# Expert weights in loads of 2 MB, a ring of eight homes and an activation in two halves, in a one-core streaming encoder step

## What is computed

```python
logits = h @ w_router + b_router
gates, experts = softmax_of_top4(logits)
for each expert e, for its tokens xe:
    gu = xe @ w_gate_up[e] + b_gate_up[e]          # (1024, 2048)
    g = jnp.minimum(gu[:, :1024], 7.0)
    u = jnp.clip(gu[:, 1024:], -7.0, 7.0)
    a = g * jax.nn.sigmoid(1.702 * g) * (u + 1.0)
    ye = a @ w_down[e] + b_down[e]                 # (1024, 1024)
x = x + sum over a token's experts of gate * ye
```

## Time and profile before

| | before |
|---|---|
| runs | 1434.07, 1432.60, 1427.69 us |
| median | 1432.6 us |
| the profiled execution's own time | 1428.79 us |
| its span | 1426.8 us |
| mean granted TensorE clock | 0.959 of full speed |
| PE / DVE / ACT busy | 1296.7 / 322.1 / 188.2 us |
| read from HBM | 439.24 MB |

### The profile page before, as it was taken

One profiled execution on the slowest core, in us unless ns is written; L12 is line 12 of the kernel. 1 busy time (PEld: TensorE's weight loads), 2 busy tenths in 40 slices (PEclk: granted clock), 3 DMA queues, 4 the chain that ended last, 5 costly groups with the idle time before them and its releaser, 6 DMA issues.

```text
span 1426.8 us, 15124 instructions
## 1 busy us (share of the span) xinstructions
PE 1296.7 (91%) x5759; PEld 597.6 (42%) x5759; DVE 322.1 (23%) x530; ACT 188.2 (13%) x344; POOL 34.5 (2%) x38
## 2 busy tenths in 40 slices
PE   5999996889988998999989899998999989899996
PEld 3445453774464434434343343434434344343432
DVE  1056004113032212312121221212312122221213
ACT  3120213220110111001010100101001010100100
POOL 4000004000000000000000000000000000000000
PEclk9999998989978999999999999999999999999999
DMA  9131421031734999999999999999999999999993
GB/s 309 59 118 59 139 83 47 2 125 61 307 129 171 379 416 411 415 410 407 410 405 416 412 414 406 406 416 419 415 420 411 413 404 416 410 414 407 403 416 141
DMA packets 89715, 443.10 MB, mean 311 GB/s; under 512 B 7971, under 2 KB 9787, under 8 KB 56414
## 3 DMA queue, kind: packets, MB, share of 16 engines
q1 hardware_dynamic: 85376, 434.94, 75.7%
q10 hardware_dynamic: 3054, 4.87, 1.0%
q0 software_dynamic: 1264, 2.99, 0.7%
HBM read 439.24 MB, written 3.53 MB: 310 GB/s over the span
## 4 chain that ended last, share of the span: by engine, by line
PE 71%; DVE 8%; issue 3%; ACT 1%; DMA 1%; DVEq 0%; SPq 0%; POOL 0%; PEldq 0%
PE bank L1385 31%; PE bank L1419 18%; PE bank L1365 7%; PE bank L1352 4%; PE bank L1237 3%; PE bank L1297 3%; DVE tu L992 1%; DVE tu L999 1%; DVE aT L1002 1%; PE bank L1406 1%; DVE tu L996 1%; DVE tg L985 1%; DMA wpool<-in_w_pool 1%; PE bank L1317 1%; PE bank L1249 1%
## 5 line engine op out<-in xcount | busy, mean ns | idle before, releaser
L1385 PE MATMUL bank<-near,xT 128*64 128x512 f32 x1280 | 284.4, 594 | 15.7 <-PE bank L1419 14.7
L1385 PEld LDWEIGHTS bank<-near,xT 128*64 128x64 f32 x1280 | 96.0, 137 | 198.7 <-issue 198.7
L959 DVE TENSOR_TENSOR x<-x,bank 128x512 f32<-128x512 f32 x102 | 70.1, 687 | 438.0 <-PE bank L1365 438.0
L1419 PE MATMUL bank<-ring,aT 128*64 128x512 f32 x768 | 168.3, 594 | 0.0
L1385 PE MATMUL bank<-ring,xT 128*64 128x512 f32 x768 | 167.5, 592 | 0.0
L1047 PE MATMUL bank<-ring,hT 128*128 128x512 f32 (+1 forms) x384 | 160.7, 578 | 1.6 <-DMA ring<-in_w_in 1.3
L1419 PE MATMUL bank<-near,aT 128*64 128x512 f32 x256 | 84.4, 821 | 45.3 <-DVE aT L1002 45.3
L1047 PEld LDWEIGHTS bank<-ring,hT 128*128 128x128 f32 x384 | 73.0, 192 | 85.5 <-issue 81.4
L1352 PE MATMUL bank<-pick,h 128*128 128x128 f32 x768 | 95.1, 282 | 9.1 <-PE bank L1385 5.9
L1385 PEld LDWEIGHTS bank<-ring,xT 128*64 128x64 f32 x768 | 55.2, 137 | 109.6 <-issue 109.6
L1352 PEld LDWEIGHTS bank<-pick,h 128*128 128x128 f32 x768 | 90.8, 197 | 22.7 <-issue 19.0
(11 more groups left out here) (247 smaller groups left out, 787.4 us busy)
## 6 DMA issues: line engine op xcount, KB each, us to landing
near<-in_w_gate_up SPq DMA_DIRECT2D x160, 1024.0 KB, 12.9
ring<-in_w_gate_up SPq DMA_DIRECT2D x96, 1024.0 KB, 9.8
ring<-in_w_down SPq DMA_DIRECT2D x96, 1024.0 KB, 12.2
near<-in_w_down SPq DMA_DIRECT2D x32, 1024.0 KB, 8.4
ring<-in_w_in SPq DMA_DIRECT2D x16, 1024.0 KB, 8.1
ring<-in_w_out SPq DMA_DIRECT2D x4, 1024.0 KB, 5.8
ring<-in_cache_k SPq DMA_DIRECT2D x2, 1024.0 KB, 6.7
ring<-in_cache_v SPq DMA_DIRECT2D x2, 1024.0 KB, 6.8
```

What stands on the lines that cost most here:

```text
L959: V.tensor_tensor(x[:, t, 512 * h:512 * h + 512], x[:, t, 512 * h:512 * h + 512], bank[6 + q % 2][:, :], ALU.add).then_inc(y_added, 1)
L1385: last = T.matmul(bank[n][64 * a:64 * a + 64, :], xT[:, w, 64 * a:64 * a + 64], slot_of(2 * w + a)[:, 512 * n:512 * n + 512], start=(w == ...
L1419: last = T.matmul(bank[4 + n][64 * a:64 * a + 64, :], aT[:, 2 * j + c, 64 * a:64 * a + 64], slot_of(k + a)[:, D * c + 512 * n:D * c + 512 ...
```

## The change

It does these things:

- **Loads.** A load is 2 MB: one piece of 16 KB per partition, for both kinds. For gate/up partition `p` gets rows 8p+2j and 8p+2j+1 (pieces of 16 KB that lie 64 KB apart in memory); for down it gets rows 4p to 4p+3 of a half (the 2 MB lie together). A pair has four gate/up steps `j` and two down steps `h`, for two experts: 12 loads.
- **Homes.** Eight homes of 2 MB: five in `near` and three in the old `ring`, and a sixth place in `near` that is used once, by load 8, since `g2row` and `sq2` stand there until the second norm is done. Six loads can go before the output projection is done, two after it, and load 8 after the norm. `unit_used` goes up by two per step, now 4 MB at a time.
- **Order of contraction.** `gather` takes the columns of `h2` with stride 8, the transposes take those of `gu` and `bgn` with stride 4, so that rows and weights meet.
- **Activation.** It is done in two halves of 512 columns; `aT` serves as the sigmoid's target too, and ACT copies three of the four banks. The last gate/up step computes its banks in the order 0, 2, 1, 3; the first transposes go before bank 3's matmuls. Each down step waits only for its own half.
- **Loop.** Turns stand in twos (`b`), the first two written out ahead of the loop. Ranks are kept once and lowered by 64 when used, in place of six copies.
- **The end.** The last two loads go in four pieces of 1 MB, by halves of the last down step. The last six combine matmuls go to banks of their own and wait for no add; `x` is written in six transfers of 256 KB. The router bias is fetched by ACT after `g2row` instead of by POOL at the start.

```diff
-DEPTH = 12
+DEPTH = 8
+LOADS = 24
+SCOL = 2 * 2048
+STREAM = [(b, j, a) for b in range(2) for j in range(6) for a in range(2)]
+GU_STEPS = 4
+        def place(k, first):
+            return k if first and k <= DEPTH else (k - 1) % DEPTH
...
+            def source(k, group, rows=4, row=0):
+                b, j, a = STREAM[k]
+                if j < GU_STEPS:
+                    return bass.AP(gu_t, group * (4 * D * 2 * FF) + ((2 * b + a) * (D * 2 * FF) + 2 * j * 2 * FF),
+                                   [[KC * 2 * FF, P], [1, SCOL]])
+                return bass.AP(dn_t, group * (4 * FF * D) + ((2 * b + a) * (FF * D) + (j - GU_STEPS) * (FF // 2) * D + row * D),
+                               [[4 * D, P], [1, rows * D]])
...
-            for k in range(DEPTH):
-                if k >= RING:
-                    sp.wait_ge(released, PRO_UNITS - RING + (k - RING) + 1)
-                load(k, 0)
+            for k in range(DEPTH + 1):
+                if 5 <= k < 8:
+                    sp.wait_ge(released, PRO_UNITS - RING + 2 * (k - 5) + 2)
+                if k == 8:
+                    sp.wait_ge(sumsq2, NT)
+                    sp.wait_ge(h2_ready, NT)
+                load(k, 0, True)
             sp.wait_ge(route_ready, 1)
             turns = turns_of(sp)
+            for k in range(DEPTH + 1, LOADS):
+                sp.wait_ge(unit_used, k - DEPTH if k <= 2 * DEPTH else k - DEPTH + 1)
+                load(k, 0, True)
...
+            for piece in range(2):
+                for a in range(2):
+                    k = LOADS - 2 + a
+                    sp.dma_start(slot_of(k, False)[:, piece * 2 * D:(piece + 1) * 2 * D],
+                                 source(k, PAIRS_E // 2 - 1, 2, 2 * piece)).then_inc(last_in[2 * piece + a], 16)
+            for q in range(2 * NT):
+                h, t = divmod(q, NT)
+                cols = slice(512 * h, 512 * h + 512)
+                dst = O[0][0, t * P:(t + 1) * P, cols] if t < 2 else O[1].rearrange("b s d -> (b s) d")[:, cols]
+                sp.wait_ge(x_done, q + 1)
+                sp.dma_start(dst, x[:, t, cols]).then_inc(out_sem, 16)
...
-                act.wait_ge(g_ready, i + 1)
-                act.wait_ge(table_set, i + 1)
-                A.activation(ts[:], tg[:], ACT.Sigmoid, scale=ALPHA).then_inc(sig_ready, 1)
-                if not final:
-                    gathered_out(i + 1, 1)
+                act.wait_ge(table_set, nth(1, 1))
+                for h in range(2):
+                    act.wait_ge(g_ready, nth(2, h + 1))
+                    A.activation(aT[:, 4 * h:4 * h + 4, :], tg[:, 4 * h:4 * h + 4, :], ACT.Sigmoid, scale=ALPHA).then_inc(sig_ready, 1)
+                    if not final:
+                        gathered_out(nth(1, 1), h)
...
-                                        h2[:, t, (4 * half + c) * P:(4 * half + c + 1) * P],
+                        last = T.matmul(bank[6 + half][:, c * P:(c + 1) * P], h2[:, t, 4 * half + c::KC],
```

More of the change, by code:

```diff
@@ L376, in _ @@
[L376 to L384, removed]
+                for k in range(LOADS):
+                    sp.wait_ge(unit_used, i * LOADS + (LOADS + k - DEPTH + 1))
+                    load(k, (i + 1) % (PAIRS_E // 2), False)
@@ L685, in _, with table_load @@
-            A.activation(table, eps, ACT.Sigmoid).then_inc(table_set, 1)
-            turn(turns, True)
+            def table_load():
+                A.activation(table, eps, ACT.Sigmoid).then_inc(table_set, 1)
+            for b in range(2):
+                table_load()
+                turn(0, 0, b, False)
+            with act.Fori(0, turns) as i:
+                for b in range(2):
+                    table_load()
+                    turn(i, 1, b, False)
+            for b in range(2):
+                table_load()
+                turn(turns, 1, b, b == 1)
@@ L931, in _ @@
             step(V.scalar_tensor_tensor(rt[:, 5, :], bank[0][:, 0:NT * E], 1.0, sel, ALU.add, ALU.mult))
-            for q in range(MAXPASS):
-                last = V.tensor_scalar(rank_all[:, q, :, :], rt[:, 5, :].rearrange("p (t e) -> p e t", t=NT), -float(q * SLOTS),
-                                       None, ALU.add)
-            step(last)
+            step(V.tensor_copy(rank[:], rt[:, 5, :].rearrange("p (t e) -> p e t", t=NT)))
             step(V.tensor_reduce(need, bank[0][:, 128:128 + E], AX.X, ALU.max))
@@ L1004, in _ @@
[L1004 to L1011 removed]
+                    dve.wait_ge(pickg_ready, nth(1, 1))
+                    pick_slots(nth(1, 1), following)
+                dve.wait_ge(gu_done, nth(4, 2))
+                V.tensor_copy(gu[:, FF:FF + 512], bank[2][:, :]).then_inc(gu_copied_v, 1)
@@ L1015, in _ @@
+            turn(turns, 1, 0, PAIRS_E // 2 - 1, PAIRS_E - 1, False)
+            turn(turns, 1, 1, PAIRS_E // 2 - 1, None, True)
         @block.tensor
@@ L1430, in turn @@
                         last.then_inc(back_turned, 1)
-                pe.wait_ge(down_done, 2 * i + 2)
-                pe.sem_inc(unit_used, 2)
+                if not final:
+                    pe.wait_ge(down_done, nth(2, 2))
+                    pe.sem_inc(unit_used, 2)
+                else:
+                    pe.wait_ge(back_ready, nth(1, 2))
+                    for q in range(6):
+                        h, t = divmod(q, NT)
+                        if q == 0:
+                            pe.wait_ge(rows_ready, nth(2, 3))
+                        if q == NT:
+                            pe.wait_ge(last_rows, 1)
+                        T.matmul(bank[LAST_BANKS[q]][:, :], back[:, t, :], y[:, 512 * h:512 * h + 512],
+                                 start=True, stop=True).then_inc(y_part, 1)
+            for b in range(2):
+                turn(0, 0, b, True, False)
             with pe.Fori(0, turns) as i:
-                turn(i, False)
-            turn(turns, True)
-            combine(turns + 1)
+                for b in range(2):
+                    turn(i, 1, b, False, False)
+            for b in range(2):
+                turn(turns, 1, b, False, b == 1)
 _CONSTANTS = {"c_keep": keep_constants, "c_mask": mask_constants, "c_rep": repeat_constants,
```

317 lines of the change are left out of this document (165 added, 152 removed).

## The result

The changed kernel takes **1448.6 us** (median of 4 runs, 1448.0 to 1450.1), the kernel before, measured beside it, 1430.5. The ratio is **1.0127** (95% interval 1.0109 to 1.0144): slower by 1.3%, where 1367 us and faster had been predicted. The profiled execution took 1448.01 us with a span of 1446.2 us, 19.4 longer than that of before. The mean granted clock rose from 0.959 to 0.977 of full speed, and the kernel still became slower.

A forecast was written before the change was run, and what follows sets the result against it. PE was taken as the bound, transfers keeping pace. Span 1426.8 − 40.1 − 3.6 − 23.8 + 4.8 + 1 − 1.9 + 2 = 1365.2 us, plus 2.0 outside it: 1367 us, range 1354 to 1390.

The forecast's parts named there:

- the predicted PE work: Expert loop: PE alone would need 57.2 us a turn after the change, less than the transfers need.
- The strided operands … So 0: Gathers and transposes on PE: loading weights with strides of 32 and 16 bytes adds 0, judged from transpose rows.
- The rival by strided weights: 64 strided PE records a turn take twice their 0.12 us: 7.7 us a turn longer, 1484 us; chance 0.01.
- Wait for `a_ready`, −40.1 us: PE's wait for the activation before down: halves remove it in fifteen turns, −40.1 us.
- The clock, −23.8 us: PE's granted clock in the loop: without the idle it no longer falls, fourteen turns × 1.70, −23.8 us.
- The rival that it falls "behind waits for data": PE's clock falls all the same, behind light gathers or data waits: 23.8 us back, 1389 us at most; chance 0.12.
- Three pieces, +0.3 us a turn: PE's transposes in a turn: one run of 16 becomes three pieces, 0.3 us a turn, +4.8 us in all.
- Routing and `bgn`, +1 us: Before the loop: fewer rank copies save about half a us, bgn's fetch beside expert loads costs +1.5; together +1 us.
- The last turn and the end: Last turn: PE's wait falls from 5.24 to about 1.6 us, −3.6, clock fall stays; end after down 9.3 us, −1.9.
- The loads, 433 GB/s and +2 us of waits: Expert loads: 16 KB pieces arrive at 433 GB/s, the lead lasts about to the end, +2 us of last-turn waits.
- from here on the transfers are the slower side: Expert loop after the change: a turn's transfers need 58.1 us, PE alone 57.2 us.
- The rival that 16 KB brings nothing: Expert loads stay at the 8 KB rate, 426 GB/s, with data waits from the middle on: 1375 us; chance 0.17.

The follow-up runs named there:

- run 1: The changed kernel, but VectorE writes h2 with its columns already sorted, so gathers and h2 transposes read neighbours; 1372.8 us, ratio 0.961.
- run 6: run 1 with the first down step waiting for both halves of aT; 1379.8 us (one run).
- run 8: run 1, but from the third pair on each load brings only half its bytes, PE's work unchanged; 1355.2 us (one run).
- run 7: run 6 with the first two groups of gu transposes moved behind the first gather; 1437.8 us (one run).
- run 5: run 1 with each 2 MB load issued as two of 1 MB, in 8 KB pieces per partition; 1390.2 us, ratio 0.9711.
- run 2: The kernel before with only its gathers changed, to read the columns of h2 with stride 8; 1458.4 us (one run).
- run 3: The changed kernel with the first gather at stride 2 and the second at stride 4; 1402.0 us (one run).
- run 9: The changed kernel with the first gather at stride 3 and the second without stride; 1376.1 us (one run).

## Why the prediction was wrong

The turns are 62.58 us, and the predicted PE work was 57.2. By its own steps:

- **The failed step: "The strided operands … So 0".** It was 6.0 us a turn, 90 us over fifteen turns, and 3.4 more for the first gather group, where the whole miss is 81.6. The rows were read rightly and carried over to the wrong thing: they give the distance between two transposes, and the strides cost next to nothing there (0.13 us apart), while a gather record went from 0.112 to 0.238 us and its load of weights from 192 to 335 ns. A hint was in the same trace, the duration of the loads: 196 ns with stride and 141 without, for transposes. It gives no price: a contiguous gather's load takes 192 ns too, and such records follow each other at 0.112 us. Why a transpose hides the stride and a gather doesn't, no run here takes apart.
- **The rival by strided weights** had the mechanism, 7.7 us a turn as price and 3.9 us as the point of decision. 6.0 was measured, and it decided as written. A chance of 0.01 was the second error: the rival was excluded by 12 records of another operation.
- **Wait for `a_ready`, −40.1 us**: right. One wait of down is left, the last turn's. That the gathers' growth covered something here was no matter, since run 1 has none either.
- **The clock, −23.8 us**: right for the changed kernel, in which the granted clock doesn't fall before the last turn, nor does it in runs 6 and 8; run 7 shows that it falls again with the idle. The rival that it falls "behind waits for data" does come true, where there are such waits. In run 1 they are 1.7 to 2.3 us long before the last turn, and behind two of the six the clock is at 0.50:

```profile
978.35 7.07 PE L1442 MATMUL bank<-near,xT 128*64 128x512 f32 x24 [2.26 <-DMA near<-in_w_gate_up]
```

```profile
980.00:983.00 3.00, 3.00 (x8) 0.91 (x6) 0.00 (x0) 0.00 (x0) 0.00 (x0) 0.50 1.03 437
```

  That costs nothing there, as the rival said ("hides part of the waits"): two turns in a row take 117.4 to 117.6 us with or without it, since the transfers set them.
- **Three pieces, +0.3 us a turn**: nothing. From 61.13 − 2.67 − 1.59 (fourteen falls over fifteen turns) = 56.87 the turns went to 56.56 in run 8, 0.3 less.
- **Routing and `bgn`, +1 us**: the gather began 1.4 us later (433.01 against 431.61), and the gap of 0.99 us behind it went, so 0.4. But the output projection had ended 1.0 us earlier, and from its end to the first gather it was 29.6 us against 27.2: 2.4 more, not 1. The wait for `bgn` was 2.44 us beside 2.31: no contention. The 48 records of the logits took 10.42 us where they had taken 8.09, and that is the clock: it is at 0.50 for all of them, where it had averaged 0.66 before, since it fell at 408.1 us instead of 413.4. Why it fell earlier stays open.
- **The last turn and the end**: the timeline has, for the changed kernel and then for run 8,

```profile
1421.37 8.78 PE L1481 MATMUL bank<-near,aT 128*64 128x512 f32 x32 [1.80 <-DVE aT L1036]
```

```profile
1330.32 7.09 PE L1487 MATMUL bank<-near,aT 128*64 128x512 f32 x32 [1.83 <-DVE aT L1042]
```

  PE waits 1.8 us where 1.6 was predicted and the earlier trace rows had 5.24. The clock falls there still (8.78 us against the 7.02 of a middle turn), as predicted, but behind the same wait in run 8 it doesn't. From the end of down, 1437.65, to the end of the span are 8.5 us, against 11.2 before and 9.3 predicted.
- **The loads, 433 GB/s and +2 us of waits**: hidden in the changed kernel (its queue waits for PE), and visible in run 1. The rate was 428 to 429, not 433. The estimate "from here on the transfers are the slower side" was right, the lead was used up at about 830 us and not at the end, and the waits cost 17.6 us in the turns and, with two falls of the clock, 6.2 in the last. Part of that may be a loop which started 7.9 us earlier in run 1 than in run 8 (436.27 against 444.13). The rival that 16 KB brings nothing falls, unless it is the number of transfers that run 5 shows: it is 17.4 us slower.

The balance of the profiled spans: the loop starts 3.8 us later, fifteen turns are 1.45 us longer each (21.8), and the last turn with the end is 6.2 shorter, 68.9 before and 62.7 after: +19.4. With the strides of `h2` out, run 1 lies at 1372.8, inside the range of 1354 to 1390: 5.8 us above the forecast. Its profiled span is 4.1 above the forecast's 1365.2: waits for data and the falls behind them +21.8 (23.8 less the 2 predicted), PE's own turns −9.6 (56.56 against 57.2), the start of the loop −5.7 (436.27 against 441.92), the last turn apart from waits −2.4 (61.0 in run 8 against 68.9 − 3.6 − 1.9). So its nearness to the forecast is in part luck: the waits were put at a tenth of what they cost, and the early start, which lies in what scatters from run to run, makes up for a quarter of that.

## What to carry to other kernels

When an edit turns a contiguous operand of a matmul into a strided one, price it on an instruction of the same kind and at the same clock, not on the nearest strided operation; where no row has one, a single edit of the kernel before (run 2) gives the price. A load of weights that takes longer with a stride is a hint. If an operand is read many times and written once (here 768 gather records and 3 writes), put the order into the write. And when a change removes a wait, count again what ran in its shadow: the same strides cost the kernel before 1.6 us a turn and the changed one 6.

The best version here is run 1: the change as it is, with `h2` written sorted, 1372.8 us.

## What the hardware showed that was not expected

- A float32 gather record of 128 rows and 128 columns takes 0.112 us with stride 1, 0.119 with 2, 0.175 with 3, 0.233 with 4 and 0.238 with 8, at 2.4 GHz; the strides are those of the operand that is loaded as weights. At 1.2 GHz it takes 0.214 with stride 1 or 3 and 0.240 with 8.
- Transposes of the same shape hardly notice: 12 with stride 8 in 1.58 us before, 12 contiguous ones in 1.50 in run 1.
- 8 KB pieces came at 421 GB/s and 16 KB pieces at 429, in the same kernel and place, with the DMA engines' share at 1.01 in both. With 16 KB pieces 64 KB apart the rate was no lower than the 426 GB/s of the contiguous 8 KB rows; what the pitch itself costs wasn't measured.
- The clock stayed at 2.4 GHz through the loop with an idle of 0.8 us a turn (run 6, up to the last turn) and fell to 1.2 GHz for a stretch of each turn with one of 3.5 us (run 7). In between the idle alone doesn't decide: behind 2.67 us it fell in 14 of 15 turns (before), behind 1.7 to 2.3 us in 2 of 6 (run 1), and behind the 1.8 us ahead of the last down step it fell in the changed kernel and in run 1, but not in runs 3, 8 and 9.
